# Moving the remainders of SBUF addresses: split weight slots 32 bytes longer, the gated products' low parts 64 bytes further

## What is computed

```
def _swiglu(h, w_in, w_out):
    g, u = jnp.split(h @ w_in, 2, axis=-1)
    return (jax.nn.silu(g) * u) @ w_out
...
        h = h + 0.5 * g1 * _swiglu(_prenorm(h, norm_ffn1[layer], sh1, sc1), ffn1_w_in[layer], ffn1_w_out[layer])
        hc = hc + 0.5 * cg1 * _swiglu(_prenorm(hc, norm_ffn1[layer], csh1, csc1), ffn1_w_in[layer], ffn1_w_out[layer])
...
    for i in range(DEPTH):
        j = i // N_MIXERS
        if i % N_MIXERS == 0:
            mix = retention(x, ret_w_in[j], ret_w_out[j])
        else:
            mix = dilated_attention(x, attn_w_in[j], attn_w_out[j], rel_bias)
        x = _layer_norm(DEEPNORM_ALPHA * x + mix, ln_gain[i, 0], ln_bias[i, 0])
        x = _layer_norm(DEEPNORM_ALPHA * x + swiglu_ffn(x, ffn_w_up[i], ffn_w_down[i]),
                        ln_gain[i, 1], ln_bias[i, 1])
```

## Time and profile before

| | |
|---|---|
| median of three runs | 2685.79 us |
| profiled execution, span | 2685.8 us |
| PE busy, share of the span | 2627.7 us, 98% |
| PEld (weight loads) busy | 2324.4 us, 87% |
| DVE, ACT, POOL busy | 1484.3, 1042.3, 199.0 us |
| mean granted TensorE clock | 0.993 |
| chain that ended last | PE 92% of the span, 91% of it at L97 |
| HBM | 402.25 MB read, 150 GB/s over the span |

### The profile page before, as it was taken

How to read it: one execution, slowest core, us unless ns; L and a number is a source line. 1 busy time by engine, 2 the same in 40 slices (tenths; PEclk the granted TensorE clock), 3 DMA queues, 4 the chain that set the end, 5 groups by cost and what they waited for, 6 DMA issues and landing times.

```text
span 2685.8 us, 40437 instructions
## 1 busy us (share of the span) xinstructions
PE 2627.7 (98%) x17444; PEld 2324.4 (87%) x17444; DVE 1484.3 (55%) x1985; ACT 1042.3 (39%) x1402; POOL 199.0 (7%) x192
## 2 busy tenths in 40 slices
PE   6999999989999999999999999999999999999998
PEld 4788888878888888888887899999999999988998
DVE  4666654746565556553364665565555554565554
ACT  3322223634212223222243554443754454455443
POOL 0000000111000010000011000010010020144001
PEclk9999999999999999999999999999999999999999
DMA  7544445115435344353262275554445466663452
GB/s 254 179 159 156 154 152 169 48 60 173 141 118 180 130 153 157 133 164 99 70 198 71 72 232 192 158 194 155 158 160 177 159 202 189 189 151 102 160 196 85
DMA packets 376080, 405.98 MB, mean 151 GB/s; under 512 B 7264, under 2 KB 352176, under 8 KB 375904
## 3 DMA queue, kind: packets, MB, share of 16 engines
q1 hardware_dynamic: 375904, 403.40, 46.5%
HBM read 402.25 MB, written 1.12 MB: 150 GB/s over the span
## 4 chain that ended last, share of the span: by engine, by line
PE 92%; DVE 3%; ACT 2%; issue 2%; POOL 1%; DMA 0%; SPq 0%; DVEq 0%; POOLq 0%; ACTq 0%
PE bank L97 91%; PE bank L100 1%; DVE w_lo L108 1%; ACT w_hi L104 1%; POOL acc L108 1%; DVE tmp L116 0%; DVE df_sc L125 0%; DMA ident<-in_ident 0%; ACT df_e L105 0%; ACT x_hi L104 0%; DVE hT L116 0%; ACT at_pT L104 0%; ACT L104 0%; DVE acc L108 0%; DMA lim<-in_limits 0%
## 5 line engine op out<-in xcount | busy, mean ns | idle before, releaser
L108 DVE TENSOR_TENSOR w_lo<-w_raw,w_hi 128x2048 fp32r<-128x2048 f32 (+2 forms) x331 | 698.0, 2112 | 765.6 <-ACT w_hi L104 765.1
L97 PE MATMUL bank<-x_hi,w_hi 128*128 128x256 f32 (+1 forms) x3000 | 988.9, 330 | 4.3 <-DVE x_lo L116 2.2
L97 PE MATMUL bank<-x_hi,w_lo 128*128 128x256 f32 (+1 forms) x3000 | 979.2, 327 | 0.0
L97 PE MATMUL bank<-x_lo,w_hi 128*128 128x256 f32 (+1 forms) x3000 | 974.1, 326 | 0.0
L104 ACT ACTIVATE w_hi<-w_raw 128x2048 fp32r<-128x2048 f32 (+2 forms) x331 | 577.9, 1750 | 383.2 <-PE bank L97 232.4
L97 PEld LDWEIGHTS bank<-x_hi,w_hi 128*128 128x128 f32 x3000 | 572.7, 191 | 65.9 <-issue 17.0
L97 PEld LDWEIGHTS bank<-x_hi,w_lo 128*128 128x128 f32 x3000 | 572.6, 191 | 47.4
L97 PEld LDWEIGHTS bank<-x_lo,w_hi 128*128 128x128 f32 x3000 | 570.3, 191 | 46.7 <-issue 0.7
L97 PE MATMUL bank<-hid_hi,w_hi 128*128 128x512 f32 (+1 forms) x1056 | 357.1, 338 | 0.0
L97 PE MATMUL bank<-hid_hi,w_lo 128*128 128x512 f32 (+1 forms) x1056 | 355.5, 337 | 0.0
L97 PE MATMUL bank<-hid_lo,w_hi 128*128 128x512 f32 (+1 forms) x1056 | 355.4, 337 | 0.0
(11 more groups left out here) (276 smaller groups left out, 2336.3 us busy)
## 6 DMA issues: line engine op xcount, KB each, us to landing
w_raw<-in_ffn_w_in SPq DMA_DIRECT2D x88, 1024.0 KB, 5.9
w_raw<-in_ada_w SPq DMA_DIRECT2D x72, 1024.0 KB, 8.0
w_raw<-in_ffn_w_up SPq DMA_DIRECT2D x44, 1024.0 KB, 5.1
w_raw<-in_attn_w_in SPq DMA_DIRECT2D x36, 1024.0 KB, 5.3
w_raw<-in_ffn_w_out SPq DMA_DIRECT2D x32, 768.0 KB, 4.7
w_raw<-in_ret_w_in SPq DMA_DIRECT2D x24, 1024.0 KB, 5.3
w_raw<-in_ffn_w_out SPq DMA_DIRECT2D x32, 640.0 KB, 4.2
w_raw<-in_odd_w_in SPq DMA_DIRECT2D x12, 1024.0 KB, 5.4
```

Source lines behind the costliest of these rows:

```text
L97: return Issued(self.eng and self.eng.matmul(out, lhsT, rhs, start=start, stop=stop, skip_group_check=loose))
L108: return Issued(self.eng and self.eng.tensor_tensor(out, a, b, op))
```

## The change

Nothing is added, removed or reordered: on every engine the same instructions stand in the same order with the same waits, and only addresses differ.

```
+SHIFT = 8
...
 def hidden(k, tag):
-    return Operand(tag, k.place("hid_hi", MID, [P, 12, 2 * T], F32R), k.place("hid_lo", MID + 24576, [P, 12, 2 * T], F32R))
+    return Operand(tag, k.place("hid_hi", MID, [P, 12, 2 * T], F32R), k.place("hid_lo", MID + 24576 + 8 * SHIFT, [P, 12, 2 * T], F32R))
...
-        k.whi, k.wlo = sb("w_hi", [P, NSPLIT, UNIT], F32R), sb("w_lo", [P, NSPLIT, UNIT], F32R)
+        k.whi, k.wlo = sb("w_hi", [P, NSPLIT, UNIT + SHIFT], F32R), sb("w_lo", [P, NSPLIT, UNIT + SHIFT], F32R)
...
-        k.sums = [k.place(f"sums{i}", MID + 49152 + 4096 * i, [P, 2, 512]) for i in range(2)]
+        k.sums = [k.place(f"sums{i}", MID + 49152 + 8 * SHIFT + 4096 * i, [P, 2, 512]) for i in range(2)]
```

## The result

Four runs of the change took 2699.51 to 2704.9 us, median 2701.76; four of the kernel before 2685.76. The ratio of the change's time to that of before is 1.0057, 95% interval [1.0045, 1.0068]: 16 us slower, where 22 us faster was forecast, and 1.8 us above the upper end of the predicted range (2700). The profiled execution is the one of 2704.9 us, 17.3 us of span above that of before.

The account below looks back on a forecast made before the run. PE's matmuls were taken to bound the kernel almost everywhere; -19.3 + 5.1 (256 columns) - 8.1 (512 columns) = -22.3 us took 2685.8 to 2663.5 us. The range was 2630 to 2700 us.

Parts of the forecast that it names:

- What bounds the kernel: Whole kernel: PE is busy 2627.7 of 2685.8 us, so only shorter matmuls or PE's few waits can move the time.
- Step (1): All engines: same instructions, order and waits; nothing is queued differently.
- Step (2): 256-column matmuls: 7150 with streams apart save 2.7 ns (-19.3 us), 2210 with equal remainders cost 2.3 more (+5.1 us).
- the `odd` stretch: Layer 1's output projection, where odd_hi lies 64 bytes from the loaded operand: 118.9 ns a matmul against 120.0.
- Step (3): 512-column matmuls: 75% of 5400 with streams apart save 2 ns, -8.1 us; equal remainders 0.
- Steps (4): ScalarE's and VectorE's splits write to other remainders but stay covered by the matmuls; costed at nothing.
- (5): sums and the rest of the work area move too, a small share of PE's time; nothing.
- Rival A: All matmuls: nothing moves, about 2686 us, the rhythm being the array's own; chance 0.22 together with D.
- Rival B: Equal-remainder matmuls behind unequal ones cost 127.3 ns, the others keep 120.0: about 2713 us; chance 0.17 with milder forms.
- Rival C: All float32r matmuls: the 13.5 ns are mostly stream collisions and come free, about 2520 us or below 2630; chance 0.07.
- the 199: All 14,760 float32r matmuls: 13.5 ns each independent of length, 199 us, the only stock an address change can draw on.
- Rival D: Addresses: moving by 32s does little if other remainders carry the weight; time as A's, chance 0.22 together with A.

Follow-up runs that it names:

- e5: Kernel before with the whole work area 192 bytes further, slots unmoved: 2681.35 us (ten runs), ratio 0.9987.
- e4: Kernel before with a pad of 32 bytes ahead of w_hi, so all operands move together: 2687.0 us against 2686.99, ratio 1.000.
- e3: Kernel before with the whole work area 64 bytes further, slots unmoved: 2669.83 us, ratio 0.9931.
- e11: Kernel before with the work area 160 bytes further, slots unmoved: one run, 2720.91 us.
- e7: Kernel before with the work area 32 bytes further, slots unmoved: one run, 2697.23 us.
- e12: As e9, but the weights' slots move 64 bytes only behind layer 1's output projection; against the kernel before: 2659.19 us, ratio 0.9885.
- e9: Against the kernel before, weights' slots begin 64 bytes further from layer 1's output projection on; 512-column products keep difference 0: 2663.68 us, ratio 0.991.
- e2: Kernel before with only hid_lo and sums 64 bytes further, slots unmoved: 2693.25 us (ten runs), ratio 1.0017.
- e13: Kernel before with 64 bytes between w_hi and w_lo, so only w_hi keeps its old remainder: one run, 2682.03 us.

## Why the prediction was wrong

- **What bounds the kernel: right.** PE's waits and the splits hardly moved, and the change of the distances reached the end: -15.3 + 28.2 = 12.9 us in the float32r matmuls, 16.8 in PE's busy time, 17.3 in the span. What lies between the first and the last is spread over other matmuls, as told above, and is not tied to the layout.
- **Step (1), the same instructions: right**, by the counts.
- **Step (2), 256 columns: right in its sum, but by luck.** It said -19.3 + 5.1 = -14.2 us; measured -15.3. The two terms were both off, and the errors cancelled: the pairs apart take 118.2 ns in the change, not 117.3, and the pairs that are equal modulo 128 take 118.7, not 122.3. "Apart" against "equal" is not the line that divides them: the map has 96 at 120.0 ns although it is apart, and nearly all the "equal" pairs of the change differ by 128, which is not 0. What the `odd` stretch did show rightly is that another difference can make this shape faster.
- **Step (3), 512 columns: wrong, and this is the step that failed.** It said -8.1 us, with bounds of -73 and +12; measured +28.2, 5.4 ns for each of 5343 distances. These 36.3 us are the whole miss; step (2) missed its sum by 1. The 2 ns came from a record without a load behind it, which showed what taking the load away gives. It was used for what moving the load gives, as if the equal layout were a collision in this shape too. The runs show the opposite: 0 is the best of seven differences. The 25% of "equal" pairs, priced at nothing, rose as well: those with a difference of 128 take 232.0 ns. Nor is a record without a load a floor for anything: in the stretch of `e5` shown above the records of 256 columns have a mean of 276 ns with a load behind each, where the prediction's record without one had 279. The upper bound was wrong as well: it carried the +2.3 ns of `odd_lo` over from 256 columns, so that a bound for one shape rested on rows of the other. The text itself said that no row had such a matmul; then the honest bound is the largest effect that any row shows, taken in either sign: the 7.3 ns between a long `odd_lo` (127.3) and 120.0, or +39 us, and the range would have held the time.
- **Steps (4) and (5): right.** The splits changed by 5 ns at most, and the distances behind the matmuls that read `sums` add up to 5.71 us before and 5.72 in the change.
- **Rival A falls.** `e4` against `e3` and `e11` shows that the difference alone moves the time between 2670 and 2721 us. The distance between two matmuls of float32r depends on where the moving and the loaded operand lie relative to each other, 114.4 to 120.0 ns with 256 columns and 226.9 to 234.3 with 512. The Trainium skill (SBUF — State Buffer, "Who interferes with whom") says that TensorE's two read ports are independent and that TensorE waits for nobody. That does not describe these two streams, and the measurement decides.
- **Rival B** had the right sign and 2712 us, but not the mechanism. It needed the pairs with equal remainders to be long, and the 75% with other remainders to be neutral. In the trace of the change the two kinds of pairs go the same way: with 512 columns both are longer (232.0 and 232.5 ns), and with 256 both are shorter in the mean (118.7 and 118.2).
- **Rival C falls.** The smallest distance of 256 columns that a stretch holds is 113.3 ns, 6.8 above the 106.5 of its columns; the largest gain of a layout for all is that of `e3`, 17 us of the 199. By the fixed part of about 2.5 ns of the Trainium skill (TensorE: Matmul & The Clock Gate, "Wait — 56ns, not 53.3ns?") an estimate for 256 columns would be 109 ns; no run here shows so small a part for this type.
- **Rival D falls.** Steps of 32 bytes matter: 32 alone (`e7`) take 512 columns from 226.9 to 233.3 ns.

**What stays open.** Why a difference of 0 suits 512 columns and not 256. A guess is that with 256 columns the load of the next operand is the limit (PEld is busy for 389.30 of 400 us in the second stretch before, for 243.99 of 300 in the first), so that a layout that speeds the load pays there, and one that slows the moving stream shows only with 512. That would fit, but it is only argued: no run changed the length of the load, or put a third length of the moving operand beside the two. Open too is why a product's three distances move together, and what picks one of the two rhythms when PE starts again at difference 192. At 4.45 ns for each of some 7200 matmuls, that choice is large enough for the 20 us by which the runs of `e5` differ, but only one run of each kernel has a trace.

## What to carry to other kernels

An effect measured on one shape of an instruction is a sample of that shape: before it is carried to another, ask whether the same thing limits both, and if no row shows the other shape, bound it from both sides by the largest effect seen anywhere. Where a kernel uses float32r matmuls back to back, the difference of the two operands' addresses is worth a map: one pad of 32 to 192 bytes moved this kernel between 2670 and 2721 us, and one run a pad, read by shape in the timeline, was enough to draw it. Only where a layout has more than one rhythm is one run not enough: look first whether the distance is the same in all long stretches. And when two phases want different layouts, each can have its own, as `e12` shows; whether it pays to switch where PE pauses anyway, `e9` and `e12` do not settle.

## What was unexpected of the hardware

- The relative place of moving and loaded operand, in steps of 32 bytes, changes the distance of two float32r matmuls by up to 5.6 ns of 120 (256 columns) and 7.4 of 227 (512); moving both together changes nothing (`e4`).
- Moving one of three operands changes all three matmuls of a product (`e2`, `e13`).
- At a difference of 192 the same addresses give two rhythms, 113.3 and 117.8 ns. One of them holds to 0.1 ns from one pause of PE to the next, over up to 1438 matmuls, and the same stretch of the program has the one in one run and the other in another. The time of the kernel spreads over 20 us in ten runs (`e5`), where thirteen runs of the kernel before beside it spread over 7.
